# One step of a two-layer decoder with experts: loads, transposes and the last expert split put in another order

## What is computed

```
x = layer_norm(ALPHA * x + h, ln1_g, ln1_b)          # h: the mixer's output
scores = sigmoid(xt @ w_router)                      # then the best 8 of 64, in 4 of 8 groups
def expert_step(acc, ew):
    wg, wu, wd, gcol = ew
    h = silu(xt @ wg) * (xt @ wu)
    return acc + gcol[:, None] * (h @ wd), None
shared = (silu(xt @ w_sg) * (xt @ w_su)) @ w_sd
x = layer_norm(ALPHA * x + acc + shared, ln2_g, ln2_b)
gate = sigmoid(x @ w_ple_gate)
x = x + gate * (p[i] @ w_ple_proj)                   # p[i]: the layer's input embedding
```

## Time and profile before

| what | value |
|---|---|
| median of 3 runs | 1689.93 us (1688.67 to 1693.67) |
| profiled execution | 1688.68 us |
| its span on the core | 1686.9 us |
| TensorE busy | 1597.2 us, 95% of the span |
| VectorE busy | 538.8 us, 32% |
| ScalarE busy | 340.6 us, 20% |
[...]
| read from memory | 526.15 MB, 326 GB/s with what is written |

### The profile page before, as it was taken

The page is one execution under the profiler, slowest core; times in us unless marked ns, Lnnn a source line. Parts: engine busy times, 40 slices in busy tenths (PEclk is TensorE's granted clock), DMA queues, the critical chain, the costliest instruction groups (busy, mean ns, idle before and its releaser), DMA issues.

```text
span 1686.9 us, 21785 instructions
## 1 busy us (share of the span) xinstructions
PE 1597.2 (95%) x7950; PEld 807.9 (48%) x7950; DVE 538.8 (32%) x1316; ACT 340.6 (20%) x689; POOL 144.6 (9%) x221
## 2 busy tenths in 40 slices
PE   7999899999999999899999999989999999999988
PEld 5784544434344443346665755454444444443333
DVE  2145722222222222351344244381222222222225
ACT  2201222111122211231222222021222112221122
POOL 0330100000000000000011011010000000000000
PEclk9969999999999999999999999989999999999999
DMA  9523779999989999954465576577999998999970
GB/s 308 231 81 125 281 314 420 421 420 420 419 352 420 420 421 420 381 175 161 151 248 191 196 266 223 201 302 294 420 420 421 420 419 361 421 420 420 420 278 28
DMA packets 119110, 536.09 MB, mean 318 GB/s; under 512 B 17816, under 2 KB 29208, under 8 KB 69247
## 3 DMA queue, kind: packets, MB, share of 16 engines
q1 hardware_dynamic: 95815, 470.35, 69.6%
q0 software_dynamic: 21360, 61.64, 10.0%
q10 hardware_dynamic: 1872, 3.22, 0.5%
HBM read 526.15 MB, written 23.87 MB: 326 GB/s over the span
## 4 chain that ended last, share of the span: by engine, by line
PE 80%; DMA 12%; DVE 4%; issue 2%; ACT 1%; SPq 1%; POOL 0%; ACTq 0%; DVEq 0%
PE ps L1228 23%; PE ps L1093 12%; DMA weights<-in_w_exp_up 11%; PE ps L1071 11%; PE ps L1242 10%; PE ps L1204 5%; PE ps L1221 3%; PE ps L1200 2%; PE ps L1235 1%; PE ps L1082 1%; PE ps L993 1%; PE ps L1262 1%; PE ps L971 1%; PE ps L886 1%; PE ps L984 1%
## 5 line engine op out<-in xcount | busy, mean ns | idle before, releaser
L1228 PE MATMUL ps<-weights,x_feat 128*64 128x512 f32 x1984 | 437.8, 593 | 36.8 <-DMA weights<-in_w_exp_up 18.5
L1228 PEld LDWEIGHTS ps<-weights,x_feat 128*64 128x64 f32 x1984 | 147.1, 137 | 320.6 <-issue 318.0
L1242 PE MATMUL ps<-weights,arena 128*64 128x512 f32 x992 | 226.5, 598 | 0.9 <-ACT arena L1423 0.9
L1071 PE MATMUL ps<-x_feat,weights 128*128 128x288 f32 x832 | 212.7, 414 | 1.1 <-ACT x_feat L1423 1.1
L1071 PEld LDWEIGHTS ps<-x_feat,weights 128*128 128x128 f32 x832 | 161.6, 196 | 46.9 <-issue 4.9
L2065 DVE CAST split<-state 128x1024 fp32r<-128x1024 f32 x64 | 44.4, 695 | 327.3 <-ACT state L1423 327.3
L2062 DVE SCALAR_TENSOR_TENSOR arena<-arena,ps 128x256 f32<-128x256 f32 x64 | 30.8, 481 | 364.8 <-ACT arena L1646 364.8
L2370 POOL DMA_INDIRECT arena<-x_rows,arena x64 | 63.6, 993 | 890.2 <-DVE arena L2055 844.4
L1423 ACT ACTIVATE state<-ps 128x512 f32<-128x512 f32 x132 | 78.8, 597 | 269.0 <-PE ps L1242 261.1
L1093 PE MATMUL ps<-weights,x_feat 128*128 128x512 f32 x288 | 127.0, 595 | 3.0 <-ACT x_feat L1449 3.0
L1242 PEld LDWEIGHTS ps<-weights,arena 128*64 128x64 f32 x992 | 65.7, 136 | 132.2 <-issue 130.9
(11 more groups left out here) (286 smaller groups left out, 1294.2 us busy)
## 6 DMA issues: line engine op xcount, KB each, us to landing
weights<-in_w_exp_gate SPq DMA_DIRECT2D x124, 1024.0 KB, 14.8
weights<-in_w_exp_up SPq DMA_DIRECT2D x124, 1024.0 KB, 18.8
weights<-in_w_exp_down SPq DMA_DIRECT2D x124, 1024.0 KB, 16.7
weights<-in_w_in_c SPq DMA_DIRECT2D x24, 1024.0 KB, 7.9
arena<-in_state_ret POOLq DMA_DIRECT2D x20, 512.0 KB, 5.6
out_ret_sample<-arena POOLq DMA_DIRECT2D x20, 512.0 KB, 6.9
weights<-in_w_in_a SPq DMA_DIRECT2D x8, 1024.0 KB, 10.5
weights<-in_w_ple_gate SPq DMA_DIRECT2D x8, 1024.0 KB, 17.6
```

Source lines behind the costliest of these rows:

```text
L1071: last = pe.matmul(ps[:, 0:T], lhs(c), XT[:, c, :], start=(c == 0), stop=(c == n - 1))
L1228: last = pe.matmul(ps[64 * s:64 * s + 64, :], XGT[u][:, c, 64 * s:64 * s + 64], rhs, start=(c == 0), stop=(c == KC - 1))
L1242: last = pe.matmul(ps[64 * s:64 * s + 64, :], HT[u][:, c, 64 * s:64 * s + 64], wd[s][:, c, 512 * n:512 * n + 512], start=(c == 0), stop=(c ...
```

## The change

Five edits. (1) At the start only the identity is loaded first, then `X` in three loads in the order of `ORD`, each with its own semaphore; the rest of the table follows the first weight panel. (2) Chunk 0 is turned and scaled before the last mixer product instead of behind it, and in the odd layer the samples come second (`ORD1`): their output product runs ahead of chunk 1's second product, and chunk 1 is the one turned behind the barrier. (3) The router's weights and bias are loaded before the barrier, into a place of their own in the arena (`EARLY`), and `PIN` is loaded first behind it. (4) `pT` and the scores run ahead of all shared products. (5) The last pair's output is split and summed by halves of 512 columns.

```diff
-    steps += [("out", 0, 1), ("norm", h, 1), ("out", 1, 0), ("out", 1, 1), ("out", 2, 0), ("out", 2, 1)]
+    steps += [("out", 0, 1), ("norm", h, 1), ("out", 1, 0), ("out", 2, 0), ("out", 2, 1), ("xtb", 0, 0), ("out", 1, 1)]
...
-            out(f"out{l}")
-        xt(f"xTb{l}", range(3))
-        g.extend(((f"router{l}",), (f"sh{l}", 0), (f"scores{l}",), (f"sh{l}", 2), (f"sh{l}", 1)))
-        g.extend(((f"cum{l}",), (f"pT{l}",), (f"sh{l}", 3), (f"lists{l}", 0), (f"lists{l}", 1), (f"flag{l}",)))
+            out(f"out{l}", (0, 1))
+            xt(f"xTb{l}", (0,))
+            out(f"out{l}", (2,))
+        xt(f"xTb{l}", ORD1[l][1:])
+        g.extend(((f"router{l}",), (f"pT{l}",), (f"scores{l}",), (f"sh{l}", 0), (f"sh{l}", 2), (f"sh{l}", 1)))
+        g.extend(((f"cum{l}",), (f"sh{l}", 3), (f"lists{l}", 0), (f"lists{l}", 1), (f"flag{l}",)))
...
-            sp.dma_start(CC[:, :], C[0]).then_inc(sem("const_in"), 16)
-            tokens(sp, X, (A["x_prompt"][0], A["x_sample"].rearrange("b s d -> (b s) d")), sem("x_in"))
+            sp.dma_start(ident, C[0][:, 0:P]).then_inc(sem("ident_in"), 16)
+            for j in ORD:
+                o, r = CH[j]
+                src = A["x_prompt"][0][o:o + r, :] if j < 2 else A["x_sample"].rearrange("b s d -> (b s) d")
+                sp.dma_start(X[0:r, j, :], src).then_inc(sem("x_in", j), 16)
...
                     panel(("qk",), split_cols(wi, 0))
+                    sp.dma_start(CC[:, P:], C[0][:, P:]).then_inc(sem("const_in"), 16)
...
+                            sp.dma_start(WR, A["w_router"][l].rearrange("(p c) n -> p (c n)", c=KC)).then_inc(sem("router_in"), 16)
+                            sp.dma_start(rbias, A["router_bias"][l:l + 1, :].broadcast_to([P, E])).then_inc(sem("rbias_in"), 16)
                             for m in range(2):
                                 expert_panel(None, E - 2, m, halves_of(HOME_UP[m]), sem("home_in"))
                             sp.wait_ge(phase_end, 4 * (2 * l + 1))
-                            sp.dma_start(WR, A["w_router"][l].rearrange("(p c) n -> p (c n)", c=KC)).then_inc(sem("router_in"), 16)
-                            sp.dma_start(rbias, A["router_bias"][l:l + 1, :].broadcast_to([P, E])).then_inc(sem("rbias_in"), 16)
+                            tokens(sp, PIN, (A["p_prompt"][l, 0], A["p_sample"][l].rearrange("b s d -> (b s) d")), sem("p_in"))
                             for f in range(2):
                                 sp.dma_start(WSD[f], A["w_sh_down"][l, P * f:P * f + P, :]).then_inc(sem("shared_down_in"), 16)
-                            tokens(sp, PIN, (A["p_prompt"][l, 0], A["p_sample"][l].rearrange("b s d -> (b s) d")), sem("p_in"))
...
                     even_pe(pe, st, begin, end, feat, tok)
+                    pe.wait_ge(sem("const_in"), 16)
...
                     for j, (o, r) in enumerate(CH):
+                        if j == 2:
+                            transpose_x(f"xTb{l}", 0, (sem("x_mid", l), 1))
...
-                for j in range(2):
-                    transpose_x(f"xTb{l}", j, (sem("x_mid", l), j + 1))
+                transpose_x(f"xTb{l}", ORD1[l][1], (sem("x_mid", l), 2))
                 st.phase()
 
-                transpose_x(f"xTb{l}", 2, (sem("x_mid", l), 3))
...
-                shared(0)
+                pe.wait_ge(sem("p_in"), 32 * (l + 1))
+                ps = begin((f"pT{l}",))
+                for f in range(2):
+                    for j in range(2):
+                        last = pe.transpose(ps[:, P * (2 * f + j):P * (2 * f + j) + P], PIN[:, j, P * f:P * f + P], ident)
+                end(last, (f"pT{l}",))
...
+                landed(pe, (f"shgu{l}",))
+                shared(0)
                 shared(2)
                 shared(1)
-                pe.wait_ge(sem("p_in"), 32 * (l + 1))
...
-                ps = begin((f"pT{l}",))
-                for f in range(2):
-                    for j in range(2):
-                        last = pe.transpose(ps[:, P * (2 * f + j):P * (2 * f + j) + P], PIN[:, j, P * f:P * f + P], ident)
-                end(last, (f"pT{l}",))
                 shared(3)
...
+                pe.wait_ge(sem("token_onehot", l), PAIRS)
+                pe.wait_ge(sem("y_split", l), PAIRS)
+                for j in range(2):
+                    end(sums(j, 0, 1, True), (f"sum{l}", j, 0))
                 for b in range(3):
                     pe.wait_ge(bank_free[b], base[b] + LOOP_USES[b])
-                pe.wait_ge(sem("token_onehot", l), PAIRS)
-                pe.wait_ge(sem("y_split", l), PAIRS)
-                for j in ORD:
-                    for n in range(2 if j < 2 else 1):
-                        end(sums(j, n, 1, True), (f"sum{l}", j, n))
+                pe.wait_ge(sem("y_split", l), PAIRS + 1)
+                end(sums(0, 1, 1, True), (f"sum{l}", 0, 1))
+                end(sums(2, 0, 1, True), (f"sum{l}", 2, 0))
+                end(sums(1, 1, 1, True), (f"sum{l}", 1, 1))
...
                         if j == 2:
+                            x_affine(f"xTb{l}", l, 1, (0,))
                             keep_strips(f"out{l}")
                         norm_root(l, 1, j, j)
-                x_affine(f"xTb{l}", l, 1, range(2))
+                x_affine(f"xTb{l}", l, 1, ORD1[l][1:2])
                 st.phase()
 
 
 
-                x_affine(f"xTb{l}", l, 1, (2,))
+                x_affine(f"xTb{l}", l, 1, ORD1[l][2:])
...
                     if kind == "out" and i:
-                        norm(1, 1, h, h, sem("x_mid", 1))
+                        norm(1, 1, ORD1[1].index(h), h, sem("x_mid", 1))
+                elif kind == "xtb":
+                    x_affine("xTb1", 1, 1, (0,))
...
+                    if last:
+                        for n in range(2):
+                            c = slice(512 * n, 512 * n + 512)
+                            if n:
+                                dve.wait_ge(bank_free[1], base[1] + uses(1, pr, 1))
+                            else:
+                                dve.wait_ge(bank_free[0], base[0] + uses(0, pr, 2))
+                            y_high(c).then_inc(sem("y_high", l), 1)
+                            dve.wait_ge(sem("y_high", l), pr + 1 + n)
+                            y_low(c).then_inc(sem("y_split", l), 1)
+                        continue
                     dve.wait_ge(bank_free[0], base[0] + uses(0, pr, 2))
-                    dve.wait_ge(bank_free[1], base[1] + uses(1, pr, 1 if last else 2 if tail else 3))
+                    dve.wait_ge(bank_free[1], base[1] + uses(1, pr, 2 if tail else 3))
...
-                x_affine(f"xTb{l}", l, 1, range(2))
+                        if j == 1:
+                            x_affine(f"xTb{l}", l, 1, (0,))
+                x_affine(f"xTb{l}", l, 1, ORD1[l][1:2])
```

51 lines of the change are left out of this document (30 added, 21 removed).

## The result

The changed kernel is faster: a median of 1683.49 us over 11 runs (1676.66 to 1686.26) against 1691.87 us over 11 runs of the kernel before (1688.67 to 1694.45). The ratio is 0.994, 95% interval 0.9929 to 0.9952. That is 8.4 us less, where 10.8 us were forecast; the median lies inside the range of 1673 to 1686 us, 4.5 us above the forecast of 1679 us. Of these 4.5 us some 1.9 are the starting point: the median of before stood at 1689.93 us with three runs and at 1691.87 us with eleven. The other 2.4 us are the size of the gain.

The account below looks back on a forecast made before the run. TensorE, busy 95% of the span, was taken as the bound, so only its waits could shrink. Terms 3.4 + 0.0 + 2.1 + 1.9 + 3.4 = 10.8 us off 1688.68 us, plus the median's 1.25 us, gave 1679 us, range 1673 to 1686 us.

Parts of the forecast that it names:

- Activations first: Start: activations land ahead of most of the table, so the first projection begins 3.4 us earlier, bounds 2.4 to 3.8.
- the 11 us that the prediction named as a sign of being wrong: Start: the gate bias was expected at about 10.7 us; landing after 11 us would show the forecast wrong.
- First barrier: Ahead of the even layer's experts: barrier 0.2 us later, weight wait frees 0.6 us; region 0.0 us, bounds -0.6 and +0.9.
- Second barrier: Odd layer: barrier 2.5 us and router 2.65 us earlier, moved transposes take 0.5 us; gain 2.1 us, bounds 1.0 and 2.6.
- Last pairs: Ends of expert loops: split and sums by halves gain 1.9 us (odd, 1.5 to 2.1), 3.4 us (even, 1.9 to 3.9).
- The first (loops give the lead back): Rival: loads bound the expert loops, early gains are waited away, only the tails' 5.3 us stay: 1684.6 us; chance 0.09.
- the second: Rival: an added register operation slows the odd layer's 22 looped pairs, each 0.1 us costing 2.2 us; chance 0.05.
- The third (the long half-clock stretch): Rival: the 26 to 34 us at half clock change; with 12 us saved 1667 us; chance 0.06.
- The fourth: Rival: nothing measurable, start gains lost to a later gate bias and tails to unseen waits, 1685 to 1690 us; chance 0.06.

Follow-up runs that it names:

- the run with samples last: Changed kernel with the odd layer's output products in the old order, samples after chunk 1 and turned behind the barrier; ratio 0.9947 to the kernel before.
- The run of the old order: Changed kernel with transposes of the embedding rows and scores back in their old places among the shared products behind the router; ratio 0.9947 to the kernel before.
- the run with a busy mixer: Changed kernel with three added, unread TensorE products (six instructions) where TensorE waits for VectorE's keys in the even mixer; ratio 0.9924 to the kernel before, median 1679.87 us.
- everything together with the old order: Changed kernel with old order behind the router, three added products at each barrier and three in the even mixer; ratio 0.9945 to the kernel before, median 1681.87 us.
- the four kernels with 12 or 14 added TensorE instructions: Changed kernel with seven added products per barrier, or three per barrier and in the even mixer, each with either router order; ratios 0.9998, 0.9996, 0.9945, 0.9926.
- the two with six: Three added products (six instructions): at each barrier with old router order, ratio 0.9934; or in the even mixer of the changed kernel, ratio 0.9924.
- the first run with seven products: Changed kernel with seven added, unread TensorE products at each barrier, new order behind the router kept; ratio 0.9998 to the kernel before.

## Why the prediction came out as it did

**Activations first: 3.4 us forecast, 2.67 us measured.** Mechanism right, size off. The step that failed is the landing of the first 128 rows at 4.3 us, worked out at 267 KB per us, the rate of 1152 KB in a row; they landed at 5.3 us, 2.65 us behind the identity (0.75 + 1.9 us), which is 193 KB per us. The last rows landed at 7.6 us, not at 6.7. The gap-free transposes and the 1.05 us behind them (1.08 us) came as worked out. The bias landed at 6.10 + 4.6 = 10.7 us, as forecast, and held nothing up. In the run with samples last it landed at 5.88 + 5.4 = 11.3 us, past the 11 us that the prediction named as a sign of being wrong, and the gap ahead of the projection was 1.28 us, so it cost 0.2 us there.

**First barrier: 0.0 us forecast, 0.5 us measured** (lead 2.67 to 3.16 us), within its bounds. The barrier itself gained 0.5 us, where a loss of 0.2 us was forecast; the weights freed 0.3 us, not 0.6; and the way from the router on, with the four transposes and the scores in it, took 0.3 us back.

**Second barrier: 2.1 us forecast, 0.6 us measured** (6.88 to 7.44 us), below the low bound of 1.0 us. This is the step that failed most. Up to the barrier it held: 2.5 us forecast, 2.63 us measured. Behind it I priced the wide chunk in place of the narrow one by VectorE's copies alone, 0.35 us; the way to the router grew by 1.10 us, 0.9 us of it transposes (1.97 us at half clock, where the narrow chunk's took 1.08 us; at full clock the wide one takes 1.16 us), 0.4 us copies, less 0.2 us that the wait for the weights had cost. So the router was 1.5 us sooner, not 2.65 us. And I priced the moved transposes at 0.5 us where the way to the first sum grew by 0.97 us. The run of the old order is 0.3 us shorter there, but the other pairs of runs in this layer differ by 0.1 us that way and 0.4 us the other; the rest, if not all, moves with the stretch at half clock (24.15 and 25.27 us for the same rows in two runs). That the clock is at half round each barrier stood in the trace of before, and I used it only for the tail.

**Last pairs: 1.9 and 3.4 us forecast, 1.80 and 3.37 us measured.** The 3.4 us of the even layer are the 1.9 us and 1.5 us for its clock, which was 0.50 from 702 to 704 us before: the sums took 3.73 us there and 2.70 us in the odd layer, and the chain had 7.37 us of projection against 6.87 us. Right in mechanism and size; the run of the halves alone gives the same ways, clock included.

**Rivals.** The first (loops give the lead back) is out: the lead goes from 3.16 to 3.48 us over the even loop and from 7.45 us (first expert product) to 7.11 us over the odd one. With that the second is out too: 0.34 us over 22 pairs is 0.02 us a pair, and the even loop moved as much the other way without the added register operation. The third (the long half-clock stretch) did not happen by the change, but the run with a busy mixer shows that it can move. The fourth is excluded by the interval (1679.9 to 1683.7 us).

**Sum.** 2.67 + 0.49 + 0.32 + 3.37 + 0.03 + 0.56 + 0.01 - 0.34 + 1.80 = 8.91 us, the terms being the steps of the lead, which is the difference of the two spans; the medians differ by 8.4 us. The forecast of 10.8 us is 1.9 us more, 0.7 us of it from the start and 1.5 us from the second barrier, less 0.5 us that the first barrier gave unforeseen.

## What to carry to other kernels

Where an engine runs dry at the end of a loop, halving the last step of its feeder was a cheap gain here, in both layers of all twelve traces (1.80 us in the odd layer of the changed kernel), the more so where the idle time had been followed by a lower clock (3.37 us in the even one). Price work that is moved next to a barrier at the clock that the trace shows there, and for every engine that touches it. A first load was better cut here, where its reader can begin on a part (1.0 to 2.1 us).

## What the runs showed that I had not expected

- The clock fell while TensorE was busy. In the run with the busy mixer it fell near 102 us (1.00 before, 0.50 from 103 us on) behind 7 us of work with one gap of 0.2 us. In the run of the old order behind the router it was 0.52 from 1006 to 1008 us (last row below), and the 16 products of the mixer's projection at 1003.54 us took 5.82 us, where the changed kernel's at 1004.22 us took 4.13 us at 1.00; ahead of them stood 16 narrow products and no idle time, in both.

```profile
1003.54 5.82 PE L1086 MATMUL ps<-x_feat,weights 128*128 128x288 f32 x16
```

```profile
1004.22 4.13 PE L1086 MATMUL ps<-x_feat,weights 128*128 128x288 f32 x16
```

```profile
1006.00:1008.00 2.00, 2.00 (x6) 1.37 (x5) 0.00 (x0) 0.00 (x0) 0.00 (x0) 0.52 0.37 145
```

- In ten of the 14 traces one or two such stretches stand in the odd mixer, near 1006 and 1071 us, and cost 1.7 us each where I priced them; in the traces of before, of the changed kernel, of the activations in two loads and of everything together with the old order there is none. Each trace is of another kernel, so that the runs of one kernel differ in this is an estimate: two such stretches make 3.4 us, which is what lies between the changed kernel's runs up to 1679.75 us and those from 1683.14 us on, at the lower mean clock.
- In the four kernels with 12 or 14 added TensorE instructions ahead of the even layer's tail, the projection behind it stopped for 1.7 to 3.4 us with nothing to wait for; in the two with six it did not. The traces show a load on a queue that the page of the profile calls `instruction` at each of these stops, one packet of 16 KB, and in all four the products go on 1.5 to 1.6 us after its end. In the first run with seven products it lasts from 702.64 to 703.66 us, and the products go on at 705.14 us (queue, then packets, MB and share between 702.6 and 703.7 us):

```profile
q8 instruction: 1, 0.02, 5.8%
```

- The same packet stands in the changed kernel's trace, from 700.08 to 701.05 us, without a stop. With 14 added instructions the stop comes behind 4 of the projection's 16, with 12 behind 5 or 6. That TensorE waits for code there fits all this, but no run changes it alone, and it is not shown.
